# Even mixer: step widths as a unit of the stream, first taps on ScalarE, sums of squares on GpSimd, staggered channel groups, new orders behind the scan and in the norm

## The reference

```
conv_val, conv_gate, z, xbc, dt = split(x @ w_in)      # 1024, 1024, 1024, 1536, 16 columns
u   = conv_val * sigmoid(conv_gate)
u   = causal_depthwise_conv(u, conv_w, conv_b)         # 31 taps per channel
u   = silu(layer_norm(u))                              # over the 1024 channels
xbc = silu(causal_depthwise_conv(xbc, ssm_conv_w, b))  # 4 taps
dt  = softplus(dt + dt_bias)                           # the step widths, 16 heads
y   = ssd_chunked(xs * dt, dt * a, bm, cm) + xs * d_skip   # the scan, 4 chunks of 128 tokens
y   = rms_norm(y * silu(z))                            # in two groups of 512 channels, g0 and g1
return concat([u, y]) @ w_out
```

## Time and profile before

| what | value |
|---|---|
| median of three runs | 2829.11 us |
| profiled execution | 2827.5 us, its span 2825.7 us |
| TensorE busy, mean granted clock | 2665.5 us (94%), 0.966 |
| VectorE, ScalarE, GpSimd busy | 1501.7, 1108.3, 403.9 us |
| weights and other reads from memory | 247.00 MB, 88 GB/s |
| slices 19 and 20 of 40 (1271 to 1413 us) | TensorE busy in tenths 6 and 8, clock 8 and 8 |

### The profile page before, as it was taken

One profiled execution on the slowest core, in us unless ns is written; L12 is line 12 of the kernel. 1 busy time (PEld: TensorE's weight loads), 2 busy tenths in 40 slices (PEclk: granted clock), 3 DMA queues, 4 the chain that ended last, 5 costly groups with the idle time before them and its releaser, 6 DMA issues.

```text
span 2825.7 us, 33699 instructions
## 1 busy us (share of the span) xinstructions
PE 2665.5 (94%) x13693; PEld 2199.6 (78%) x13693; DVE 1501.7 (53%) x2577; ACT 1108.3 (39%) x1822; POOL 403.9 (14%) x291
## 2 busy tenths in 40 slices
PE   7999799999999999896899999999999999999998
PEld 6776567878888987784787778889788886888887
DVE  3376867355333269897865553332643753642334
ACT  2446344244332232444355353322542453542223
POOL 0031223110100033441310110000100100111000
PEclk6999899899999999998899999999999999999998
DMA  8343223433333323211342223333231241333331
GB/s 224 100 107 82 71 67 102 121 104 90 97 91 95 98 68 90 67 46 52 89 121 64 57 81 97 96 91 101 65 83 52 81 136 38 91 96 92 95 97 60
DMA packets 482298, 251.31 MB, mean 89 GB/s; under 512 B 14558, under 2 KB 479026, under 8 KB 482143
## 3 DMA queue, kind: packets, MB, share of 16 engines
q1 hardware_dynamic: 479556, 242.49, 30.5%
q0 software_dynamic: 1872, 5.66, 0.7%
q10 hardware_dynamic: 715, 1.01, 0.1%
HBM read 247.00 MB, written 2.13 MB: 88 GB/s over the span
## 4 chain that ended last, share of the span: by engine, by line
PE 77%; DVE 15%; ACT 6%; issue 1%; DMA 0%; POOL 0%; SPq 0%; DVEq 0%; ACTq 0%; POOLq 0%
PE ps L909 18%; PE ps L911 18%; PE ps L913 18%; DVE ps L2377 4%; PE ps L845 2%; PE ps L841 2%; PE ps L843 2%; PE ps L935 2%; PE ps L869 1%; PE ps L1349 1%; PE ps L859 1%; PE ps L861 1%; PE ps L1064 1%; DVE hT L3091 1%; DVE w_r L2244 1%
## 5 line engine op out<-in xcount | busy, mean ns | idle before, releaser
L909 PE MATMUL ps<-XH,wh 128*128 128x512 f32 (+1 forms) x1888 | 766.7, 406 | 13.7 <-ACT arena_f L1679 6.1
L913 PE MATMUL ps<-XH,w_r 128*128 128x512 f32 (+1 forms) x1888 | 751.5, 398 | 4.8 <-DVE w_r L2244 2.9
L911 PE MATMUL ps<-XL,wh 128*128 128x512 f32 (+1 forms) x1768 | 706.8, 400 | 3.3 <-DVE XL L2761 2.8
L2244 DVE TENSOR_TENSOR w_r<-w_f,wh 128x1024 fp32r<-128x1024 f32 (+1 forms) x315 | 377.2, 1200 | 569.9 <-ACT wh L1493 569.8
L1493 ACT ACTIVATE wh<-w_f 128x1024 fp32r<-128x1024 f32 (+2 forms) x406 | 410.4, 1014 | 391.4 <-PE ps L913 214.2
L909 PEld LDWEIGHTS ps<-XH,wh 128*128 128x128 f32 (+1 forms) x1888 | 358.8, 190 | 123.0 <-issue 19.4
L913 PEld LDWEIGHTS ps<-XH,w_r 128*128 128x128 f32 (+1 forms) x1888 | 357.5, 189 | 92.8 <-DVE w_r L2244 5.1
L911 PEld LDWEIGHTS ps<-XL,wh 128*128 128x128 f32 (+1 forms) x1768 | 335.4, 190 | 85.5 <-issue 3.6
L911 PE MATMUL ps<-arena_r,wh 128*128 128x512 f32 (+1 forms) x944 | 349.2, 370 | 4.1 <-DVE arena_r L2485 3.0
L909 PE MATMUL ps<-arena_r,wh 128*128 128x512 f32 (+1 forms) x734 | 271.7, 370 | 21.9 <-ACT arena_r L1520 11.2
L913 PE MATMUL ps<-arena_r,w_r 128*128 128x512 f32 (+1 forms) x734 | 264.6, 360 | 2.7 <-DVE w_r L2244 1.5
(11 more groups left out here) (371 smaller groups left out, 3810.9 us busy)
## 6 DMA issues: line engine op xcount, KB each, us to landing
w_f<-in_mlp_w SPq DMA_DIRECT2D x126, 512.0 KB, 4.1
w_f<-in_w_ff SPq DMA_DIRECT2D x63, 512.0 KB, 4.1
w_f<-in_w_in SPq DMA_DIRECT2D x49, 512.0 KB, 3.9
w_f<-in_ada_w SPq DMA_DIRECT2D x35, 512.0 KB, 4.0
w_f<-in_even_w_in SPq DMA_DIRECT2D x35, 512.0 KB, 3.8
w_f<-in_odd_w_in SPq DMA_DIRECT2D x23, 512.0 KB, 3.8
w_f<-in_even_w_out SPq DMA_DIRECT2D x16, 512.0 KB, 4.0
w_f<-in_xa_w_v SPq DMA_DIRECT2D x16, 512.0 KB, 4.2
```

Source lines behind the costliest of these rows:

```text
L909: e.matmul(b, hi[:, k, :], xh, start=u.first and k == 0, stop=False)
L911: e.matmul(b, hi[:, k, :], xl, start=False, stop=False)
L913: last = e.matmul(b, lo[:, k, :], xh, start=False, stop=u.final and k == u.kc - 1)
L2244: e.tensor_tensor(flat(u, 1), flat(u, 0), high_flat(u).bitcast(F32), ALU.subtract).then_inc(dve.sem, dve.up("low", u.n))
```

## The change

- The step widths become a unit `dt` of 16 columns in "ev gv", in the split form of all others, with its turn to token rows by four small transposes; `wsmall`, its DMA on GpSimd's queue and the 64 matmuls go. The cumulating matmuls come behind six units of the stream. VectorE's chain for `dt` stands in slot 3 with eight taps between its operations (`step_widths`), `nacs` and `dte` in slot 6.
- Tap 0 of each long group is made by ScalarE (`conv_first`), and so is the first tap of each 4-tap convolution ("short first"). VectorE has 30 taps a group, 240 in all.
- The groups no longer run in pairs from the same start: the next group begins 6 or 28 taps into the one before. Slots: 6 taps in the lead, 8 in each of 14 gv slots, 3 in eight xbc units, 3 a scan step, 2, 5 or 3 behind the units of y lead and y out, 7 in a new place "conv wait". Groups end in gv slots 5, 6 and 13, xbc unit 0, scan steps 10 and 12, the last slot of y out, and "conv wait".
- The sums of squares of the long convolution go to GpSimd; tile 7 is left out of both sums and added by TensorE as a second matmul.
- Behind the scan the g0 statistics come before z7's tanh on ScalarE; VectorE takes inputs 4 to 6 and two norms before z7; TensorE makes chunks 0 and 1 of the first two units, the g1 sum, chunks 2 and 3, and only then the products with the low parts. The low part of the third lead unit goes to VectorE.
- Three memory units come before the channel sums ("conv wait"), nine stay in the norm. There XH and XL of tile k-1 are made within the loop.

```diff
@@ -306,7 +306,9 @@
...
     plans["ev gv"] = after_norm("ev", units)
+    plans["ev gv"].insert(1, Unit("dt", 0, [even[:, EV_DT:EV_DT + SSM_HEADS]], "X3"))
@@ -328,8 +330,9 @@
...
+    plans["conv wait"] = [next(kv) for _ in range(3)]
     for k in range(KC):
-        plans["conv norm", k] = [next(kv) for _ in range(2 if k < 4 else 1)]
+        plans["conv norm", k] = [next(kv) for _ in range(1 if k else 2)]
@@ -398,6 +401,7 @@
...
         u.low = "pool"
+    plans["y lead"][2].low = "dve"
     plans["project parts"] = [project[:2]] + [[u] for u in project[2:]]
@@ -730,15 +733,24 @@
...
-        taps = [(m0 + j, t) for m0 in range(0, KC, 2) for t in range(CONV_W) for j in range(2)]
-        tap_slots = {("gv", i): 9 for i in range(13)} | {("xbc", m): 2 for m in XBC_ORDER[:8]}
-        tap_slots |= {("scan", st): 2 + st % 2 for st in STEPS} | {("y out", m): 10 for m in range(KC)}
+        taps = [(0, t) for t in range(1, CONV_W)]
+        for m in range(1, KC):
+            ahead = 6 if m % 2 else 28
+            at = (m - 1) * (CONV_W - 1) + ahead
+            taps[at:] = [v for t in range(1, CONV_W) for v in ([(m - 1, t + ahead)] if t + ahead < CONV_W else []) + [(m, t)]]
+        tap_slots = {("gv", "lead"): 6} | {("gv", i): 8 for i in range(14)} | {("xbc", m): 3 for m in XBC_ORDER[:8]}
+        tap_slots |= {("scan", st): 3 for st in STEPS}
+        out_items = plans["y lead"] + plans["y out"]
+        tap_slots |= {("y out", i): 0 if isinstance(u, Step) else 3 if u.name != "yout" else 2 if i < 3 else 5
+                      for i, u in enumerate(out_items)}
+        tap_slots["conv wait",] = (CONV_W - 1) * KC - sum(tap_slots.values())
@@ -1201,21 +1215,16 @@
...
-            w.wait_ge(*freed)
-            w.wait_ge(d_wdt, "wdt")
-            w.wait_ge(dve, "h", "r1n", KC - 1, 1)
-            for c in range(NT):
-                for k in range(KC):
-                    last = e.matmul(b[:, c * 16:(c + 1) * 16], hT[:, k, c * P:(c + 1) * P], wsmall[:, k, :],
-                                    start=k == 0, stop=k == KC - 1)
-            last.then_inc(pe.sem, pe.up("dt"))
+            gate_units = plans["ev gv"]
+            run_units(gate_units[:3])
+            flush()
+            run_units(gate_units[3:6])
...
+            run_units(gate_units[6:])
@@ -1302,14 +1311,51 @@
...
+            def group_products(k, low):
...
+                for u in lead[:2]:
+                    b = lin.of(*u.out) if k or low else bank_of(u)
+                    hi, lo = chunks(high_flat(u), u.kc, u.cols), chunks(flat(u, 1), u.kc, u.cols)
+                    xh, xl = chunk_of(u, k)
+                    w.wait_ge(act, "high", u.n)
+                    if low:
+                        w.wait_ge(dve, "xl", u.x, k)
+                        e.matmul(b[:, :], hi[:, k, :], xl, start=False, stop=False)
+                    else:
+                        w.wait_ge(act, "xh", u.x, k)
+                        e.matmul(b[:, :], hi[:, k, :], xh, start=k == 0, stop=False)
+                        w.wait_ge(low_by[u.low], "low", u.n)
+                        e.matmul(b[:, :], lo[:, k, :], xh, start=False, stop=False)
+            for k in range(2):
+                group_products(k, False)
+            rms_sums("g1", 4)
+            for k in range(2, 4):
+                group_products(k, False)
+            for k in range(4):
+                group_products(k, True)
             products(lead[2:], 0)
-            rms_sums("g1", 4)
...
+            run("conv wait")
...
+            e.matmul(m_sum[:, :], ones[:, :], acc_s, start=True, stop=False)
+            w.wait_ge(pool, "sumq", "conv", KC - 2)
+            e.matmul(q_sum[:, :], ones[:, :], conv_q, start=True, stop=False)
+            w.wait_ge(act, "conv out", KC - 1)
+            e.matmul(m_sum[:, :], ones[:, :], conv[:, KC - 1, :], start=False, stop=True).then_inc(pe.sem, pe.up("m", "conv"))
+            w.wait_ge(act, "sq", "conv", KC - 1)
+            e.matmul(q_sum[:, :], ones[:, :], sq_rings["conv"].of("conv", KC - 1), start=False, stop=True).then_inc(
+                pe.sem, pe.up("q", "conv"))
@@ -1653,6 +1701,8 @@
...
+                    w.wait_ge(act, "raw", m)
+                    copy(b, b, "short first", m, scale=column("even_ssm_conv_w_2", (SSM_CONV - 1) * XBC_C + m))
@@ -1901,6 +1951,16 @@
...
+            def conv_first(m):
...
+                w.wait_ge(dve, "val", m)
+                w.wait_ge(dve, "half taps")
+                copy(conv_bank[m % 2][:, :], val[:, m, 0:S], "first", m, scale=conv_tap(0, m))
...
                         act.sem, act.up("sq", "conv", m))
+                    if m + 2 < KC:
+                        conv_first(m + 2)
@@ -1924,12 +1986,19 @@
...
-            log1p_exp_minus(dt_, sc1, sc2, sc3, "dt")
-            w.wait_ge(dve, "dte")
-            e.activation(dte, dte, ACT.Exp).then_inc(act.sem, act.up("dte"))
+            conv_first(0)
             for i, u in enumerate(plans["ev gv"]):
                 run_steps([u])
+                if i == 0:
+                    conv_first(1)
+                if i == 3:
+                    flush()
+                    log1p_exp_minus(dt_, sc1, sc2, sc3, "dt")
+                if i == 6:
+                    w.wait_ge(dve, "dte")
+                    e.activation(dte, dte, ACT.Exp).then_inc(act.sem, act.up("dte"))
                 conv_out("gv", i)
@@ -1988,29 +2057,35 @@
...
+                if st == STEPS[-1]:
+                    round_ahead(plans["scan", st][0].n)
+                    rms("g0", 4 * P, 1, stat[:, 2, :])
...
+            group_high(0)
+            group_high(1)
+            for j in range(3):
+                group_square(1, j)
+            group_high(2)
+            group_high(3)
+            group_square(1, 3)
+            e.preload_act_table_set("natural_log")
             round_ahead(plans["y lead"][0].n)
-            rms("g0", 4 * P, 1, stat[:, 2, :])
-            for j in range(4):
-                group_high(j)
-                group_square(1, j)
...
-                        if u.name == "yout":
-                            conv_out("y out", u.m)
-                    steps = steps[take:]
+            run_steps(out_items[:2])
+            for i in range(2, len(out_items)):
+                run_steps(out_items[i:i + 1])
+                for n in (0, 1, 2) if i == 2 else (i,):
+                    conv_out("y out", n)
+            run_steps(plans["conv wait"][:2])
+            conv_out("conv wait")
+            run_steps(plans["conv wait"][2:])
             lin.free(act, "conv")
@@ -2364,18 +2443,12 @@
...
                 o = conv_bank[m % 2][:, :]
-                if t == 0:
-                    if m < 2:
-                        w.wait_ge(*(lin, att4)[m].held("conv"))
-                    else:
-                        w.wait_ge(act, "sq", "conv", m - 2)
-                    w.wait_ge(dve, "val", m)
-                    w.wait_ge(dve, "half taps")
-                    e.tensor_scalar(o, val[:, m, 0:S], conv_tap(0, m), None, ALU.mult).then_inc(dve.sem, dve.up())
+                if t == 1:
+                    w.wait_ge(act, "first", m)
                 else:
                     w.wait_ge(dve, tapped[m])
@@ -2820,62 +2893,72 @@
...
+            def step_widths(taps):
+                def fill(n):
+                    for _ in range(n):
+                        long_tap(*taps.pop(0))
...
+                fill(2)
...
+                e.tensor_scalar(sc2, sc1, 1.0, None, ALU.add).then_inc(dve.sem, dve.up("one plus", "dt"))
...
+                e.reciprocal(sc2, sc2).then_inc(dve.sem, dve.up("dt over"))
+                fill(1)
...
+                e.tensor_scalar(adt, adt, -1.0, None, ALU.mult).then_inc(dve.sem, dve.up("adt"))
+                fill(len(taps))
...
                 run_steps([u])
-                conv_taps("gv", i)
+                if i == 3:
+                    step_widths(list(slot_taps["gv", i]))
+                elif i == 6:
+                    b = att4.of("cumulated")
+                    w.wait_ge(pe, "cumulated")
+                    e.tensor_scalar(nacs, b[:, 0:64], -1.0, None, ALU.mult).then_inc(dve.sem, dve.up("nacs"))
+                    conv_taps("gv", i)
+                    w.wait_ge(dve, "nacs")
+                    e.tensor_tensor(dte, b[:, 64:128], nacs, ALU.add).then_inc(dve.sem, dve.up("dte"))
+                    att4.free(dve, "cumulated")
+                else:
+                    conv_taps("gv", i)
@@ -2994,41 +3071,43 @@
...
+                if st == STEPS[-1]:
+                    for m in range(4, 7):
+                        group_input(m)
+                else:
+                    run(("scan", st))
                 for m, t in slot_taps["scan", st][2 if st + 1 in STEPS else 0:]:
                     long_tap(m, t)
-                squared.extend(conv_ends["scan", st])
-            group_inputs(1)
+            group_norm(0)
+            group_norm(1)
+            run(("scan", STEPS[-1]))
+            group_input(7)
+            group_norm(2)
```

(21 more changed lines are left out.)

198 lines of the change are left out of this document (90 added, 108 removed).

## The result

The changed kernel takes 2796.41 us (median of four runs, 2795.34 to 2799.48) against 2829.15 us (2829.11 to 2831.35): ratio 0.9883, 95% interval 0.9871 to 0.9895, 32.7 us faster. The forecast was 2790, 39.2 us faster. The profiled execution is the one of 2796.68 us, its span 2794.9.

A forecast was written before the change was run, and what follows sets the result against it. TensorE is busy 2665.5 of 2825.7 us, so time comes only from its waits and slow running. 17.6 - 0.6 - 4 + 8.9 + 7.3 + 10.0 = 39.2 us, so 2829.1 - 39.2 = 2790, range 2770 to 2812.

The forecast's parts named there:

- Step widths and channel units: Stage 1015.4:1171.7, 156.3 us: becomes 133.7 + 5 = 138.7, the 5 charged at the first group end; 17.6 us gained.
- First taps: Twenty first taps leave VectorE, 13 us, and cost ScalarE 0.6 to 0.7 us each, where it has room.
- from VectorE's side: Cross-check of the sum by VectorE's earlier start and saved work: taps end about 37 us earlier than 1391.
- Prelude and scan: Up to the scan 0.6 us lost to one more ScalarE copy; scan 4 lost, with 48 taps for 40.
- Behind the scan: Stage 1293.8:1330.1, 36.3 us: g0 statistics before z7's tanh, start 3.2 us after the edge, 27.4 us; 8.9 gained.
- y out and sums: Stage 1330.1:1399.2, 69.1 us: fewer taps owed, VectorE ready in yout slots; 61.8 us, 7.3 gained.
- Norm: Stage 1399.2:1438.2, 39.0 us: nine units instead of twelve, wait before "out" ends; 29.0 us, 10.0 gained.
- The squares' sums: Seven adds leave VectorE, six of about 1.27 us go to GpSimd, whose queue has room: nothing more than charged.
- A: Each of eight staggered group ends stalls TensorE as a pair end does now: 49 us, time 2831; chance 0.10.
- B: VectorE bounds the scan and the norm: scan loses 12 instead of 4, norm gains 3 instead of 10; 2805; chance 0.20.
- C: VectorE's backlog never shows: without the charges of 5, 4, 3.0 and 3 of the 8; 2775; chance 0.17.
- D: Port hits: six GpSimd adds each hold a critical VectorE product for 1.27 us, 7.6 us; 2798; chance 0.08.

The follow-up runs named there:

- e5: Changed kernel with the step widths as before: 64 small matmuls and the whole chain ahead of the units, no unit for them; 2804.83 us.
- e2: Changed kernel with the eight long and twelve short first taps on VectorE again instead of ScalarE; 2797.44 us.
- e4: Changed kernel with 40 taps in the scan instead of 48, the eight others one more in each yout slot; 2791.75 us.
- e6: Changed kernel with the g0 statistics on ScalarE behind z7's tanh and VectorE's first two g0 norms behind z7's value, as before; 2800.01 us.
- e7: Changed kernel with the halved copies XH and XL all behind the channel norm's loop, as before, nine units still beside the norm; 2794.93 us.
- e3: Changed kernel with the six sums of channel squares on VectorE at the head of the next slot, none on GpSimd; 2802.67 us.
- e1: Changed kernel with the taps of the channel groups in pairs again, two ends in one slot; first taps stay on ScalarE; 2795.79 us.

## Why the prediction came out as it did

**What bounds the kernel: right.** The time came from TensorE's waits and the clock behind them. Its own work fell by 5.8 us.

**Step widths and channel units, 17.6 forecast, 13.7 measured.** The unit in place of the 64 small matmuls is worth 8.2 us of the stage (e5), and no wait is left in it. The charge of 4 + 1 us at the first group end measured 5.0, at the place named. Two terms were mis-sized. The pace: 0.230 us a matmul came from 174 starts in 40 us, while the starts of three in a row are 0.23 to 0.24 apart (1058.70, 1058.93, 1059.17), 0.2325 on average in 1040:1080 before, so 24 units are 24 x 24 x 0.0025 = 1.4 us more. And the charge left out the clock behind the wait: 1062:1075 has 25 starts and a granted 0.74, partly the lower level of 1.2 GHz; 57 starts were due, the other 32 are 7.4 us, 5.0 of them waits and 2.4 the lower clock.

**First taps, 13 us off VectorE and 0.6 to 0.7 us each on ScalarE, "where it has room": the step that failed.** The copies are cheap (0.69 us), but VectorE now waits for them in its own order (15.8 us for the 6.6 of e2), and at the first group end one stands ahead of the rounding for 0.8 us, so nothing is gained (e2: stretch +0.1). The check "from VectorE's side", 37 us earlier, was built on these 13: its last tap starts at 1364.2 for 1390.8, 26.6 earlier.

**Prelude and scan, 4.6 lost forecast, 6.4 measured.** The eight taps cost 2.5 us (e4), under the 4 charged, and TensorE's wait for the last decay (L2980), 4.2 us for 2.6 before, with a lower clock behind it (0.85 in 1277:1289), is part of these 2.5. Not forecast: 0.9 more in the prelude, and some 2 us that e4 still has over the kernel before from the scan's start to z7's end (98.2 for 95.9), which no run explains.

**Behind the scan, 8.9 and 10.4.** The start was 2.9 us behind z7 (3.2 forecast) and the g1 sum waited 2.2 (1.6 forecast): the step is right, and 3.0 us of it, net, is the order of the g0 statistics (e6). Mis-sized is the lower clock, 3.2 us forecast: beside 19.4 of work and these two waits the 25.9 us leave 1.4 for it.

**y out and sums, 7.3 and 9.4.** The stall at the third waiting unit is there, 3.3 us for a forecast of 3.0; no wait for a rounding over 0.4 us is left of the 9.4. The stage came out 2.1 under the forecast's 61.8. The term that was too large is the sums, 4.1 + 1.9 us: from 1371.36 to the norm's second matmul at 1374.91 they take 3.6. The 2.0 for small waits was about right.

**Norm, 10.0 and 10.7.** Right, and e7 gives its parts: 1.5 us the copies, the rest fewer units. But where the wait of 2.4 us before "out" was to end, 1.5 of them come back behind the edge, as the two waits of 0.6 and 1.3.

**The squares' sums, "nothing more than charged".** The adds on GpSimd cost nothing there, as said. What leaving VectorE is worth was put at 8.6 us of VectorE's time and weighed in no stage; e3 measures 6.5 us of the stretch.

**The rivals.** A is false: group ends cost 5.0 once, not 49, and in e1 the second pair end costs nothing. B and C are off by the measured stages, D has the wrong sign (e3). That the total came within 7 us of the forecast is in part luck: the first stage fell 3.9 us short and y out came out 2.1 better by a term that was mis-sized.

**What no term had: 7.0 us outside the table's stages.** In three places of unchanged code TensorE runs at a lower granted clock. Two of them, as windows of the same length from the same instruction on, before (first fence) and after (second):

```profile
1482.00:1518.00 36.00, 32.03 (x216) 28.50 (x215) 25.69 (x62) 24.65 (x44) 2.47 (x2) 1.00 0.21 60
2274.00:2304.00 30.00, 27.87 (x235) 27.46 (x235) 16.66 (x18) 20.61 (x34) 0.00 (x0) 1.00 0.56 161
```

```profile
1448.00:1484.00 36.00, 32.02 (x207) 28.25 (x206) 25.13 (x59) 23.92 (x43) 2.47 (x2) 0.95 0.21 59
2240.00:2270.00 30.00, 27.75 (x222) 27.35 (x221) 16.52 (x17) 19.29 (x32) 0.00 (x0) 0.94 0.53 156
```

Each costs 1.4 to 1.5 us, the third, near 2346, 1.7; before has one of its own near 2030, which gives 1.5 back. The other 1.5 us are the two waits in the first matmuls of "out". The start of the stage lies anywhere from 1015.4 to 1019.0 in the fourteen profiles of this study, and the last 6000 matmuls, from the first start to the last, take 1158.3 us in the profile before and 1158.3 to 1162.4 in the thirteen of changed kernels (1160.1 in the changed kernel itself), mostly in steps of about 1.6. So the profile that the sum was made in was at the favourable end of both. Why a given execution gets the lower clock at one of these places is open; no run tests it.

**Open.** The parts that were taken back one by one come to about 19 us of the stretch (e5 6.8, e3 6.5, e6 3.0, e7 1.5, e1 1.0, e2 0.1), of the 36.5 by which it is shorter. The rest is not shown by an experiment of its own: the taps' new slots and their earlier start, which take the wait of 9.4 us out of y out, are argued from the stages. Whether a kernel with the first taps on neither engine's critical order exists wasn't tried, nor a wait-free first group end. e4, 2791.75 us at a ratio of 0.9868, is faster than the kernel before, and its stretch is 2.7 us shorter than the changed kernel's; the intervals of the two ratios overlap.

## What to carry to other kernels

Work that goes from a full engine to one with room can be worth nothing where the full engine waits for its result in order: price the hand-over wait beside the duration saved, or place something else between. A stall at the end of a group was here the lateness of the engine ahead of it in that slot, so look there first, and expect that a wait taken away brings up the next one within a few us. Compare stages by the same instructions at both edges: most repeat to 0.2 us where whole runs differ by 3, but one here had two values 1.6 apart.

## What the runs showed of the hardware

- A VectorE sum of two operands in SBUF took 2.38 us beside a GpSimd low part of 2.40 that had started 0.6 us earlier, and 0.69 at best; on GpSimd the same sum took 1.27 to 1.30.
- The same TensorE instructions ran at a granted clock of 1.00 in one profile and 0.94 or 0.95 over 30 to 36 us in another, in stretches that the change doesn't touch. At 1.4 to 1.7 us each, that is as much as many an edit is worth.
- An idle of TensorE of 3.3 us at 1063 and 2.1 at 1067 was followed by 2.4 us lost to the lower level of 1.2 GHz (granted 0.74 in 1062:1075): these two waits cost about half as much again as they lasted.
